# The opening, the window attention and the latent scores of an fp32 two-block kernel, rearranged together

## The chip, the cores and the metric

The kernel runs on one core of one Trainium2 chip. Its time is the device time of one execution in microseconds (us), the median of several runs. TensorE (PE) multiplies, VectorE (DVE) and ScalarE (ACT) do the elementwise work, GpSimd (POOL) some of it, and SyncE (SP) issues most of the transfers. PE's results lie in PSUM, in eight banks of 128 x 512 fp32 numbers.

## The reference

Two transformer blocks over 512 tokens of 1024 channels, all in fp32. The parts that the change touches:

```python
def rmsnorm(x, g):
    y = xf * lax.rsqrt(jnp.mean(xf * xf, axis=-1, keepdims=True) + NORM_EPS)
    return (y * g.astype(jnp.float32)).astype(x.dtype)
...
    h = jnp.concatenate([meta, x], axis=1)                   # 16 + 512 tokens
    h = h + 0.5 * swiglu(rmsnorm(h, ffn1_norm[i]), ffn1_w1[i], ffn1_w3[i], ffn1_w2[i])
    hn = rmsnorm(h, mix_norm[i])
    q, k, v, u, g_attn, g_ssm = jnp.split(hn @ w_in[i], SPLITS, axis=-1)
    attn = sliding_window_attention(q, k, v, attn_sinks[i])  # 16 heads of 64, window 128
...
def mla_mixer(...):                                          # 16 heads, queries in blocks of 128
    q_rope = apply_rope(q[..., MLA_NOPE:], cos[:, :, None], sin[:, :, None])
    k_rope = apply_rope(k_r, cos, sin)
...
        s = (jnp.einsum('bqhd,bkhd->bhqk', q_nope[:, q0:q1], k_nope[:, :q1])
             + jnp.einsum('bqhr,bkr->bhqk', q_rope[:, q0:q1], k_rope[:, :q1])).astype(jnp.float32) * scale
        s = jnp.where(mask[:, None], s, NEG_INF_2)
        pr = jax.nn.softmax(s, axis=-1).astype(v.dtype)
        outs.append(jnp.einsum('bhqk,bkhd->bqhd', pr, v[:, :q1]))
```

The rest (a state-space branch, gated FFNs with a convolution, a second, gated linear attention, layer norms and projections) is the same before and after.

## The kernel before

**Products.** The channels lie on the partitions, the tokens along them. A product of two fp32 matrices is made of three matmuls of fp32r operands, high by high, low by high and high by low part (`mm3`, L566 to L568). The weights of one output chunk of 128 columns, 8 input chunks deep, are a unit (128 x 1024); a raw tile (128 x 8 x 256) holds two. 24 matmuls (8 input chunks of three) make one 512-token output chunk in one bank, and 48 make the 528-token chunks of the first FFN, in two halves of 264. SP brings each raw tile into one of three raw buffers (`loads`, L501), ACT writes its high part `uh` (`feed_hi` or `ahead_hi`, L539), DVE the low part `ul` (`feed_lo` or `ahead_lo`, L554), and PE waits for both. "Ahead" means that a unit is prepared before the one in turn.

**Order.** Each engine has its own function for each stage (`..._pe`, `..._act`, `..._dve`, `..._sp`), and these write the engine's instructions in the order in which they run. Banks are taken in rotation by `Banks.take`; a taker waits until the last holder of the bank was read. `bk.limit(n, i)` makes the rotation run over n banks, from bank i on.

**Opening** (`setup_pe`, `setup_act`, `setup_dve`, `setup_sp`). The norm's gain rows of several layers come by nine transfers on ACT's queue into tile 0 of `vrows`, and PE turns all 112 at once into columns (`columns_pe`, L888). SP brings the input `xin` in eight pieces, four token blocks by two halves of the columns, with a semaphore for each block, then the first weights. PE turns the meta tokens (L902) and the eight input chunks (L908), DVE copies each to `H` (L933), ACT writes the gained high part `XH` (L813) and squares it (L772), DVE the low part `XL` (L820). After the fourth chunk ACT and DVE split the first two units (L539, L554). Only after all the transposes does PE begin the first unit, then the sums of squares (L751); ACT takes the root (L759), DVE the inverse (L766), and the first results are scaled out of the banks (L836).

**Window attention** (`window_pe`, `window_act`, `window_dve`). Sixteen attention steps (four groups of four heads, four query blocks n) run in a loop over i = 0 to 19: scores of i (`scores_pe`, L1756), softmax of i-1 (L1769, L1773 on DVE, L1786 on ACT), normalising of i-2 (L1803), turning of i-3 (`turn_pe`, L1821; copies L1837 on ACT and L1839 on DVE), values of i-4 (`values_pe`, L1850, and L1866 on DVE). Beside them the units for the queries of groups 1 to 3 and for their gates (`q`, `ga`), at the twelve steps of `WITH_UNIT`, and one unit `gs` at i = 17: each whole unit stands ahead of the turning and the scores of its step, and its result is scaled by L836. The banks 0 to 3 rotate, 4 to 7 hold the four heads' scores.

**Latent attention** (`latent_pe` and its fellows). Two heads are a pair p. Queries and keys of a pair come from three products (`queries_pe`: `qn`, `qr`, `kn`), ACT copies QN and KN out of the banks (L2282, L2286), DVE turns the rotary part (`rope_dve`: four copies of 32 partitions each, L2174, and three multiplications and additions, L2176 to L2180). The scores of a head (`latent_scores_pe`) are two fp32 matmuls for each query block n, of N = 128(n+1) keys: QN by KN (L2319) and the rotary rows of that head, QR by KR (L2320). Softmax is L2335 and L2338 on DVE, L2345 on ACT; turning is L2367, the values are L2395, and their output goes out by ACT (L2405) and DVE (L2409). The loop runs over i = 0 to 17, one head a step and a new pair at each even step.

## Time and profile before

| | us |
|---|---|
| median of three runs (2744.53 to 2750.54) | 2745.61 |
| the profiled execution | 2743.8 |
| its span, first to last instruction | 2742.0 |
| PE busy in it | 2676.6 |
| VectorE busy | 1674.5 |
| ScalarE busy | 1015.2 |
| GpSimd busy | 348.2 |

Times below are microseconds from the start of that span. The stages on its axis: the opening up to 44.2, the first FFN, the projections and the state-space branch up to 565.4, the window attention from 565.4 to 734.2, the rest of the first block and its FFN up to 1289.9 with the latent attention's first products at its end, the latent attention's loop from 1289.9 to 1578.8, and the rest up to 2742.0. A line "L566" is line 566 of the kernel. PEclk is the TensorE clock that was granted, as a share of full speed (1.00 is 2.4 GHz, 0.5 is 1.2 GHz). What stands in brackets behind an instruction is the idle time of its engine ahead of it and what ended that. The mark PEld is the weight load of a matmul, which runs beside the matmul ahead.

### The profile page before, as it was taken

The numbers are of one execution on the slowest core, as the hardware profiler recorded it, in microseconds if no ns is written. First come the engines' busy times: TensorE is split into PE (matmuls) and PEld (weight loads), VectorE is DVE, ScalarE is ACT, GpSimd is POOL, SyncE is SP. The second block draws the span as 40 slices with busy tenths as digits, with TensorE's granted clock in tenths as the row PEclk, the third lists the DMA queues.
The fourth block names the chain that finished last, engine by engine and source line by source line (L and its number), as shares of the span: only waits on it lengthen the run. The fifth ranks groups of instructions, "written<-read, shape, count | busy, mean of one in ns | idle before, by whom it ended". The sixth has DMA issues, their size and how long they took to land.

```text
span 2742.0 us, 35232 instructions
## 1 busy us (share of the span) xinstructions
PE 2676.6 (98%) x14595; PEld 2244.8 (82%) x14595; DVE 1674.5 (61%) x2553; ACT 1015.2 (37%) x1625; POOL 348.2 (13%) x361
## 2 busy tenths in 40 slices
PE   6999999988899999999999999999999999999999
PEld 6999999866687888887667688888887878888887
DVE  6754755668556544546664667737764467764765
ACT  3321333134334222333442435424454244542435
POOL 1133423020001000011000040000221014000031
PEclk9999999999899999999999999999999999999999
DMA  5243344421132233322111132332322212232231
GB/s 144 77 123 108 104 137 126 167 74 33 33 108 96 92 100 108 89 77 66 43 65 47 58 100 78 90 103 77 114 95 85 85 46 70 85 108 92 90 103 62
DMA packets 292727, 244.02 MB, mean 89 GB/s; under 512 B 19837, under 2 KB 285575, under 8 KB 292567
## 3 DMA queue, kind: packets, MB, share of 16 engines
q1 hardware_dynamic: 282503, 226.40, 26.1%
q0 software_dynamic: 5616, 13.22, 1.6%
q8 instruction: 115, 1.88, 0.3%
q10 hardware_dynamic: 4448, 2.16, 0.3%
q14 instruction: 45, 0.37, 0.0%
HBM read 230.70 MB, written 13.14 MB: 89 GB/s over the span
## 4 chain that ended last, share of the span: by engine, by line
PE 87%; DVE 8%; ACT 2%; issue 1%; DMA 1%; POOL 1%; ACTq 0%; SPq 0%; POOLq 0%; DVEq 0%
PE ps L566 26%; PE ps L567 25%; PE ps L568 25%; PE ps L2320 2%; PE ps L2319 2%; DVE ul L554 2%; PE ps L751 1%; PE ps L2395 1%; DVE rbuf L766 1%; PE ps L2367 1%; ACT S L1786 1%; ACT uh L539 1%; PE ps L3116 1%; PE ps L3092 1%; DVE tmp L2174 1%
## 5 line engine op out<-in xcount | busy, mean ns | idle before, releaser
L554 DVE TENSOR_TENSOR ul<-raw,uh 128x1024 fp32r<-128x1024 f32 (+3 forms) x416 | 526.5, 1289 | 340.5 <-ACT uh L539 340.1
L566 PE MATMUL ps<-OH,uh 128*128 128x512 f32 (+1 forms) x1736 | 646.6, 372 | 3.6 <-DVE ul L554 2.4
L568 PE MATMUL ps<-OH,ul 128*128 128x512 f32 (+1 forms) x1736 | 638.7, 368 | 0.0
L567 PE MATMUL ps<-OL,uh 128*128 128x512 f32 (+1 forms) x1736 | 638.5, 368 | 0.0
L539 ACT CAST uh<-raw 128x1024 fp32r<-128x1024 f32 (+3 forms) x416 | 411.9, 1025 | 158.3 <-PE ps L568 128.6
L566 PEld LDWEIGHTS ps<-OH,uh 128*128 128x128 f32 x1736 | 327.3, 189 | 66.6 <-issue 7.3
L567 PEld LDWEIGHTS ps<-OL,uh 128*128 128x128 f32 x1736 | 327.4, 189 | 55.2 <-issue 2.4
L568 PEld LDWEIGHTS ps<-OH,ul 128*128 128x128 f32 x1736 | 327.3, 189 | 54.6
L566 PE MATMUL ps<-XH,uh 128*128 128x264 f32 (+1 forms) x992 | 314.1, 317 | 13.4 <-DVE ul L554 8.1
L567 PE MATMUL ps<-HL,uh 128*128 128x512 f32 (+2 forms) x946 | 320.3, 339 | 0.0
L566 PE MATMUL ps<-HH,uh 128*128 128x512 f32 (+2 forms) x946 | 320.1, 338 | 0.0
L568 PE MATMUL ps<-HH,ul 128*128 128x512 f32 (+2 forms) x946 | 318.9, 337 | 0.0
L567 PE MATMUL ps<-XL,uh 128*128 128x264 f32 (+1 forms) x992 | 309.5, 312 | 0.0
L568 PE MATMUL ps<-XH,ul 128*128 128x264 f32 (+1 forms) x992 | 308.6, 311 | 0.0
L566 PEld LDWEIGHTS ps<-XH,uh 128*128 128x128 f32 x992 | 191.5, 193 | 31.1 <-DVE ul L554 8.8
L568 PEld LDWEIGHTS ps<-XH,ul 128*128 128x128 f32 x992 | 191.7, 193 | 9.1
L567 PEld LDWEIGHTS ps<-XL,uh 128*128 128x128 f32 x992 | 191.5, 193 | 8.5
L566 PEld LDWEIGHTS ps<-HH,uh 128*128 128x128 f32 x946 | 177.8, 188 | 22.8 <-issue 0.9
L567 PEld LDWEIGHTS ps<-HL,uh 128*128 128x128 f32 x946 | 177.7, 188 | 20.8 <-issue 0.5
L568 PEld LDWEIGHTS ps<-HH,ul 128*128 128x128 f32 x946 | 177.9, 188 | 19.7
L782 POOL TENSOR_TENSOR acc<-acc,tmp 128x512 f32<-128x512 f32 (+2 forms) x56 | 70.3, 1255 | 697.6 <-ACT tmp L772 693.1
L2552 POOL TENSOR_TENSOR acc<-H 128x512 f32<-128x512 f32 x4 | 8.6, 2149 | 974.3 <-DVE H L2791 623.2
(434 smaller groups left out, 3710.8 us busy)
## 6 DMA issues: line engine op xcount, KB each, us to landing
raw<-in_ffn_w SPq DMA_DIRECT2D x40, 1024.0 KB, 5.0
raw<-in_ffn_w_up SPq DMA_DIRECT2D x40, 1024.0 KB, 5.0
raw<-in_ffn_w SPq DMA_DIRECT2D x32, 704.0 KB, 4.3
raw<-in_ffn_w_down SPq DMA_DIRECT2D x32, 704.0 KB, 4.3
raw<-in_w_in SPq DMA_DIRECT2D x16, 1024.0 KB, 5.4
raw<-in_gla_w_in SPq DMA_DIRECT2D x12, 1024.0 KB, 5.0
raw<-in_mla_w_o SPq DMA_DIRECT2D x8, 1024.0 KB, 4.8
raw<-in_ple_w_gate SPq DMA_DIRECT2D x8, 1024.0 KB, 4.9
```

The costliest lines, as they stand in the source:

```text
L539: e.copy(h, src).then_inc(*s_whi.up((u, j)))
L554: e.tensor_tensor(l, src, h.bitcast(F32), SUB).then_inc(*s_wlo.up(("unit", u)))
L566: e.matmul(o, wh, xh, start=first, stop=False)
L567: e.matmul(o, wh, xl, start=False, stop=False)
L568: return e.matmul(o, wl, xh, start=False, stop=last)
L751: i = e.matmul(psum[:, b, 0:n], ones[:, :], tile[:, t0:t0 + n], start=j == 0, stop=j == len(parts) - 1)
L766: e.reciprocal(r[:, t0:t0 + n], r[:, t0:t0 + n]).then_inc(*s_dv.up((tag, "r", hf)))
L782: e.tensor_tensor(a, a, tmps[k - 1][:, t0:t0 + n], ADD).then_inc(*s_pool.up(*((tag, "acc", k, hf) for hf in hfs)))
L1786: e.activation(S_[:, r, 0:ntot], S_[:, r, 0:ntot], ACT.Exp, bias=z[:, 1, r:r + 1], accum_out=z[:, 3, r:r + 1]).then_inc(*s_fn.up())
L2174: e.tensor_copy(s[32 * k:32 * k + 32, :], P(key, 512, slice(32 * (k ^ 1), 32 * (k ^ 1) + 32))).then_inc(*s_dv.up())
L2319: e.matmul(psum[:, b, 0:N], QN[:, hh, 128 * n:128 * n + 128], KN[:, hh, 0:N], start=True, stop=False)
L2320: e.matmul(psum[:, b, 0:N], QR[p0:p0 + 64, 128 * n:128 * n + 128], KR[p0:p0 + 64, 0:N], start=False, stop=True).then_inc(*s_mm.up(("ms", h ...
```

## The change

**1, the opening.** The first norm's gain gets an 8-row tile of its own (`g1row`, turned to `g1`), whose transfer is the first on ACT's queue; the other rows of tile 0 are turned later, in `norm()`, with tiles 1 to 3. The input has one semaphore for each half of its columns in place of one for each token block. SP brings the first half, the meta tokens, the first weight, the second half and the second weight. ACT runs one small activation ahead of its work. PE turns chunks 0 and 1, the meta tokens, chunks 2 and 3, and then takes the first unit input chunk by input chunk, with the turning of chunks 4 to 7 between. The splitting of the first unit is one unit long, the second unit is split after the last chunk. After the sums of squares the banks start again at 0 of 8.

**2, the window attention.** The units are no longer whole: `along_pe` runs them in pieces of input chunks, `CHUNKS[i]` of them at step i, those that go on with a begun unit ahead of the turning, those that begin one behind the scores (`lin_piece`). They have bank 3 alone, and 0 to 2 rotate for the rest. `gs` is the last of them. DVE adds up the values (i-4) ahead of normalising (i-2), and splits the next unit ahead of the copy from the turning or behind it (`soon`).

**3, the latent scores.** Each pair of fp32 matmuls becomes five of fp32r: three for the plain part (high and low of QN and KN) and two for the rotary part, QA by the high and the low part of KR, where QA holds the high part of the head's rotary query in one half of its partitions and the low part in the other. N is at least 256. ACT writes the high parts (QNH, KNH, QA) and takes over the four copies of the rotary part (`rope_act`); DVE subtracts for the low parts (QNL, KNL, QA's other half). KR is split once.

The diff, cut to its core:

```diff
+def lin_piece(e, name, X, t0, n, key, bank, k0, k1):
+    xh, xl, tag = X
+    if k0 == 0:
+        piece_of[key] = next_unit(e, name)
+        bk.take(e, key, bank)
+    u = piece_of[key]
+    hi, lo, _ = halves_of(u)
+    for k in range(k0, k1):
+        s_lo.wait_ge(e, (tag, k))
+        i = mm3(e, psum[:, bk.of[key], 0:n], hi[:, k, :], lo[:, k, :], xh[:, k, t0:t0 + n],
+                xl[:, k, t0:t0 + n], k == 0, k == 7)
+    if k1 == 8:
+        i.then_inc(*s_mm.up(key, ("unit", u)))
+piece_of = {}
...
         cs = slice(512 * half, 512 * half + 512)
         for i in range(4):
...
+            loads(e, 1)
     loads(e, 2)
...
+def turn_input_pe(e, c):
+    b = bk.take(e, ("xt", c))
+    d_x[c // 4].wait_ge(e, "x")
+    for i in range(4):
+        t = e.transpose(psum[:, b, i * 128:(i + 1) * 128], xin[:, i, c * 128:(c + 1) * 128], ident[:, :])
+    t.then_inc(*s_mm.up(("xt", c)))
...
 def setup_pe(e):
     s_cst.wait_ge(e, "ident")
-    columns_pe(e, 0)
+    b = bk.take(e, "g1")
+    d_g1.wait_ge(e, "row")
+    e.transpose(psum[:, b, 0:8], g1row[:, :], ident[0:8, 0:8]).then_inc(*s_mm.up("g1"))
+    for c in range(2):
+        turn_input_pe(e, c)
     b = bk.take(e, "xm")
...
-    for c in range(8):
-        b = bk.take(e, ("xt", c))
-        for i in range(4):
-            d_x[i].wait_ge(e, c // 4)
-            t = e.transpose(psum[:, b, i * 128:(i + 1) * 128], xin[:, i, c * 128:(c + 1) * 128], ident[:, :])
-        t.then_inc(*s_mm.up(("xt", c)))
+    for c in range(2, 4):
+        turn_input_pe(e, c)
+    u = next_unit(e, "f1")
+    keys = [("F1", "a", 0, hf) for hf in range(2)]
+    for key in keys:
+        bk.take(e, key)
+    hi, lo, _ = halves_of(u)
+    for k in range(8):
+        if k < 4:
+            turn_input_pe(e, 4 + k)
+        s_lo.wait_ge(e, ("ffn1", k))
+        for (t0, n), key in zip(H1, keys):
+            i = mm3(e, psum[:, bk.of[key], 0:n], hi[:, k, :], lo[:, k, :], XH[:, k, t0:t0 + n],
+                    XL[:, k, t0:t0 + n], k == 0, k == 7)
+            if k == 7:
+                i.then_inc(*s_mm.up(key, *([("unit", u)] if key == keys[1] else [])))
...
 def setup_act(e):
+    e.dma_start(g1row[:, :], r8(A["ffn1_norm"][0])).then_inc(*d_g1.up("row"))
...
-    s_dv.wait_ge(e, ("col", 0))
+    s_cst.wait_ge(e, "ones")
+    e.activation(misc[:, 3:4], one, ACT.Identity, scale=one).then_inc(*s_fn.up())
+    s_dv.wait_ge(e, "g1")
...
+    ahead_hi(e, 1)
...
-    s_dv.wait_ge(e, ("col", 0))
...
+        if c == 4:
+            feed_lo(e, "f1", 0)
...
-        if c == 5:
-            feed_lo(e, "f1")
...
+    ahead_lo(e, 1)
...
-        for tile in range(1, 4):
+        bk.limit(8, 0)
+        for tile in range(4):
             columns_pe(e, tile)
...
+ALONG = [("q" if n < 2 else "ga", 2 * g + n % 2) for g in range(1, 4) for n in range(4)] + [("gs", 0)]
+CHUNKS = (8, 8, 8, 7, 7, 7, 6, 6, 6, 6, 6, 6, 5, 5, 5, 3, 2, 2, 1, 0)
+def pieces_of(i, rest):
+    a = sum(CHUNKS[:i])
+    b = a + CHUNKS[i]
+    x = [(u, max(a - 8 * u, 0), min(b - 8 * u, 8)) for u in range(len(ALONG)) if a < 8 * u + 8 and b > 8 * u]
+    return [p for p in x if (p[1] > 0) == rest]
+def begun(i):
+    return [ALONG[u] for u, _, _ in pieces_of(i, False)]
+def ended(i):
+    x = (pieces_of(i - 1, False) if i else []) + pieces_of(i, True)
+    return [ALONG[u] for u, _, k1 in x if k1 == 8]
+def soon(i):
+    return sum(k1 - k0 for _, k0, k1 in pieces_of(i, True)) < 3
+def along_pe(e, i, rest):
+    for u, k0, k1 in pieces_of(i, rest):
+        name, c = ALONG[u]
+        lin_piece(e, name, MIX, 16, 512, (name, c, 0), 3, k0, k1)
...
-    bk.limit(4)
+    bk.limit(3)
...
-        if q_ga(i):
-            name, c = q_ga(i)
-            lin(e, name, MIX, HR, (name, c))
...
+        along_pe(e, i, True)
         if 3 <= i <= 18:
             turn_pe(e, i - 3)
         if i < 16:
             scores_pe(e, i)
+        along_pe(e, i, False)
...
+        if 3 <= i <= 18 and soon(i):
+            turn_copy(e, i - 3, True)
...
+        for name, c in ended(i - 1) if i else ():
+            ga_act(e, name, c)
+        for name, c in begun(i):
+            feed_hi(e, name)
+        if 3 <= i <= 18 and not soon(i):
             turn_copy(e, i - 3, True)
...
+        if i >= 4:
+            values_dve(e, i - 4)
...
-        if i >= 4:
-            values_dve(e, i - 4)
-        if q_ga(i):
-            feed_lo(e, q_ga(i)[0])
-        if i == 17:
-            feed_lo(e, "gs")
+        if not soon(i):
+            for name, c in begun(i):
+                feed_lo(e, name)
+        for name, c in ended(i):
+            if name == "gs":
+                scale_dve(e, ("gs", 0, 0), tmps[0][:, 0:512], rmix, ("gs in", 0))
+            else:
+                q_ga_dve(e, name, c)
         if 3 <= i <= 18:
             turn_copy(e, i - 3, False)
-        if i == 17:
-            scale_dve(e, ("gs", 0, 0), tmps[0][:, 0:512], rmix, ("gs in", 0))
-        if q_ga(i):
-            q_ga_dve(e, *q_ga(i))
+        if soon(i):
+            for name, c in begun(i):
+                feed_lo(e, name)
...
+def rope_act(e, key):
     s_mm.wait_ge(e, key)
+    if key[0] == "qr" and key[1] > 2:
+        s_dv.wait_ge(e, ("rope", "qr", key[1] - 3, 0))
+    for k in range(4):
+        e.copy(rope_tile(key)[32 * k:32 * k + 32, :], P(key, 512, slice(32 * (k ^ 1), 32 * (k ^ 1) + 32))).then_inc(
+            *s_cp.up(("rope",) + key))
...
-        e.copy(QN[:, hh, :], P(("qn", p, hh, 0))).then_inc(*bk.free(s_cp, ("qn", p, hh, 0), ("qn", p, hh)))
-    feed_hi(e, "uk", 1 if p == 1 else 2)
+        e.copy(QNH[:, hh, :], P(("qn", p, hh, 0))).then_inc(*s_hi.up(("qn", p, hh)))
+    rope_act(e, ("qr", p, 0))
...
+        e.copy(KNH[:, hh, :], P(("kn", p, hh, 0))).then_inc(*s_hi.up(("kn", p, hh)))
...
+def queries_turned_act(e, p):
+    s_dv.wait_ge(e, ("rope", "qr", p, 0))
+    for hh in range(2):
+        rows = slice(64 * hh, 64 * hh + 64)
+        e.copy(QA[rows, hh, :], QR[rows, :]).then_inc(*s_hi.up(("qr", p, hh)))
+    feed_hi(e, "uk", 1 if p == 1 else 2)
...
-            s_dv.wait_ge(e, ("rope", "qr", p - 3, 0))
...
+        s_lo.wait_ge(e, "KR")
+    for hh in range(2):
+        s_hi.wait_ge(e, ("qn", p, hh))
+        e.tensor_tensor(QNL[hh][:, :], P(("qn", p, hh, 0)), QNH[:, hh, :].bitcast(F32), SUB).then_inc(
+            *bk.free(s_lo, ("qn", p, hh, 0), ("qn", p, hh)))
...
+        s_hi.wait_ge(e, ("kn", p, hh))
+        e.tensor_tensor(KNL[:, hh, :], P(("kn", p, hh, 0)), KNH[:, hh, :].bitcast(F32), SUB).then_inc(
...
+def queries_turned_dve(e, p):
+    for hh in range(2):
+        rows, other = slice(64 * hh, 64 * hh + 64), slice(64 - 64 * hh, 128 - 64 * hh)
+        s_hi.wait_ge(e, ("qr", p, hh))
+        e.tensor_tensor(QA[other, hh, :], QR[rows, :], QA[rows, hh, :].bitcast(F32), SUB).then_inc(
+            *s_lo.up(("qr", p)))
...
-    p, hh, p0 = h // 2, h % 2, 64 * (h % 2)
-    s_cp.wait_ge(e, ("kn", p, 1))
-    s_dv.wait_ge(e, ("rope", "qr", p, 0))
-    s_dv.wait_ge(e, "KR")
+    p, hh = h // 2, h % 2
...
+    s_lo.wait_ge(e, "KR")
+    s_lo.wait_ge(e, ("qr", p))
     for n in range(4):
-        N = 128 * (n + 1)
+        N = max(128 * (n + 1), 256)
         b = bk.take(e, ("ms", h, n), 4 + n)
-        e.matmul(psum[:, b, 0:N], QN[:, hh, 128 * n:128 * n + 128], KN[:, hh, 0:N], start=True, stop=False)
-        e.matmul(psum[:, b, 0:N], QR[p0:p0 + 64, 128 * n:128 * n + 128], KR[p0:p0 + 64, 0:N], start=False,
-                 stop=True).then_inc(*s_mm.up(("ms", h, n), ("ms", h)))
+        o, q = psum[:, b, 0:N], slice(128 * n, 128 * n + 128)
+        mm3(e, o, QNH[:, hh, q], QNL[hh][:, q], KNH[:, hh, 0:N], KNL[:, hh, 0:N], True, False)
+        e.matmul(o, QA[:, hh, q], KRH[:, 0:N], start=False, stop=False)
+        e.matmul(o, QA[:, hh, q], KRL[:, 0:N], start=False, stop=True).then_inc(
+            *s_mm.up(("ms", h, n), ("ms", h)))
```

How the change stands in the engines' order. A row is a line of the kernel, the operation, result<-operands and the result's shape, with the count where rows repeat.

**The first places on PE.** Before, from its first instruction (`vrows` are the gain rows, `xme` the meta tokens, `xin` the input, `uh` and `ul` the parts of the first weight):

```order
L888 MATMUL ps<-ident,vrows 128x112
L902 MATMUL ps<-ident,xme 128x16 x8
L908 MATMUL ps<-ident,xin 128x128 x32
L566 MATMUL ps<-XH,uh 128x264
L567 MATMUL ps<-XL,uh 128x264
L568 MATMUL ps<-XH,ul 128x264
L566 MATMUL ps<-XH,uh 128x264
```

After (`g1row` is the first norm's own row tile):

```order
L933 MATMUL ps<-ident,g1row 128x8
L924 MATMUL ps<-ident,xin 128x128 x8
L939 MATMUL ps<-ident,xme 128x16 x8
L924 MATMUL ps<-ident,xin 128x128 x12
L572 MATMUL ps<-XH,uh 128x264
L573 MATMUL ps<-XL,uh 128x264
L574 MATMUL ps<-XH,ul 128x264
L572 MATMUL ps<-XH,uh 128x264
L573 MATMUL ps<-XL,uh 128x264
L574 MATMUL ps<-XH,ul 128x264
L924 MATMUL ps<-ident,xin 128x128 x4
L572 MATMUL ps<-XH,uh 128x264
```

Four of the input chunks went from ahead of the first product to between its steps of six matmuls; the meta tokens stand behind two chunks.

**SP's queue at the start**, before and after:

```order
L846 DMA xin<-in_x 128x512 x4
L848 DMA xme<-in_meta_tokens 16x1024
L846 DMA xin<-in_x 128x512 x4
L501 DMA raw_49<-in_ffn_w 128x8x256
L501 DMA raw_50<-in_ffn_w 128x8x256
```

```order
L869 DMA xin<-in_x 128x512 x4
L871 DMA xme<-in_meta_tokens 16x1024
L507 DMA raw_49<-in_ffn_w 128x8x256
L869 DMA xin<-in_x 128x512 x4
L507 DMA raw_50<-in_ffn_w 128x8x256
```

One weight tile went ahead of the second half of the input.

**DVE at step 4 of the window attention**, from the scores of step 3's softmax (`S`) to the state-space side work (`U`); `Mg` is the attention's output, `PT` the turned weights, `Q` the scaled query. Before:

```order
L1769 SCALAR_TENSOR_TENSOR S_121<-ps,mk_123 128x1088
L1773 TENSOR_REDUCE sst<-S_121 128x4
...
L1803 TENSOR_TENSOR S_128<-S_120,sst 128x4x16
L1803 TENSOR_TENSOR S_120<-S_120,sst 128x4x128
L1866 SCALAR_TENSOR_TENSOR Mg<-Mg,ps 128x128 x2
L554 TENSOR_TENSOR ul<-raw_50,uh 128x1024
L1839 COPY PT<-ps 128x512
L836 TENSOR_TENSOR Q<-ps,mbuf 128x512
L1702 SCALAR_TENSOR_TENSOR U<-U,cv,tmp_62 128x8x66
```

After:

```order
L1842 SCALAR_TENSOR_TENSOR S_123<-ps,mk_125 128x1088
L1846 TENSOR_REDUCE sst<-S_123 128x4
...
L1939 SCALAR_TENSOR_TENSOR Mg<-Mg,ps 128x128 x2
...
L1876 TENSOR_TENSOR S_130<-S_122,sst 128x4x16
L1876 TENSOR_TENSOR S_122<-S_122,sst 128x4x128
L560 TENSOR_TENSOR ul<-raw_50,uh 128x1024
L859 TENSOR_TENSOR Q<-ps,mbuf 128x512
L1912 COPY PT<-ps 128x512
L1756 SCALAR_TENSOR_TENSOR U<-U,cv,tmp_62 128x8x66
```

The adding of the values went ahead of the normalising, and the result of the unit ahead of the copy from the turning.

**DVE at a new pair of heads in the latent attention** (`ps` is a bank, `tmp` the rotary part's tile). Before:

```order
L554 TENSOR_TENSOR ul<-raw_50,uh 128x512
L554 TENSOR_TENSOR ul<-raw_51,uh 128x512
L2174 COPY tmp_62<-ps 32x512 x4
L2176 TENSOR_TENSOR QR<-ps,COS 128x512
L2178 TENSOR_TENSOR tmp_62<-tmp_62,SIN 128x512
L2180 TENSOR_TENSOR QR<-QR,tmp_62 128x512
L554 TENSOR_TENSOR ul<-raw_49,uh 128x4x256
L554 TENSOR_TENSOR ul<-raw_49,uh 128x4x128
L2409 TENSOR_TENSOR OL<-ps,OH 128x512
L2387 COPY PTm<-ps 128x512
```

After:

```order
L560 TENSOR_TENSOR ul<-raw_50,uh 128x512
L560 TENSOR_TENSOR ul<-raw_51,uh 128x512
L2394 TENSOR_TENSOR QNL_158<-ps,QNH 128x512
L2394 TENSOR_TENSOR QNL_159<-ps,QNH 128x512
L2258 TENSOR_TENSOR tmp_58<-ps,COS 128x512
L2260 TENSOR_TENSOR tmp_62<-tmp_62,SIN 128x512
L2262 TENSOR_TENSOR tmp_58<-tmp_58,tmp_62 128x512
L2399 TENSOR_TENSOR KNL<-ps,KNH 128x512 x2
L2521 TENSOR_TENSOR OL<-ps,OH 128x512
L2406 TENSOR_TENSOR QA<-tmp_58,QA 64x512 x2
L560 TENSOR_TENSOR ul<-raw_49,uh 128x4x256
```

The four copies left DVE; six subtractions came, four of them of 128 x 512 and two of 64 x 512, and the output's subtraction (`OL`) stands between them.

**PE at a head's scores.** Before, six of eight:

```order
L2319 MATMUL ps<-KN,QN 128x128
L2320 MATMUL ps<-KR,QR 128x128
L2319 MATMUL ps<-KN,QN 128x256
L2320 MATMUL ps<-KR,QR 128x256
L2319 MATMUL ps<-KN,QN 128x384
L2320 MATMUL ps<-KR,QR 128x384
```

After, the first seven of twenty:

```order
L572 MATMUL ps<-KNH,QNH 128x256
L573 MATMUL ps<-KNL,QNH 128x256
L574 MATMUL ps<-KNH,QNL_158 128x256
L2431 MATMUL ps<-KRH,QA 128x256
L2432 MATMUL ps<-KRL,QA 128x256
L572 MATMUL ps<-KNH,QNH 128x256
L573 MATMUL ps<-KNL,QNH 128x256
```

Five matmuls stand where two stood, and the narrowest has 256 columns.

## Rows read from the trace of the kernel before

**Rows 1.** The page: busy time of each engine.

```profile
PE 2676.6 (98%) x14595; PEld 2244.8 (82%) x14595; DVE 1674.5 (61%) x2553; ACT 1015.2 (37%) x1625; POOL 348.2 (13%) x361
```

**Rows 2.** By stage: length, busy of PE, PEld, DVE, ACT, POOL, PEclk, DMA.

```profile
0.00:44.20 44.20, 23.46 (x124) 21.49 (x124) 23.61 (x30) 17.13 (x24) 11.54 (x19) 0.85 0.64 175
...
565.40:734.20 168.80, 146.05 (x795) 105.88 (x793) 120.43 (x245) 67.92 (x203) 8.33 (x16) 0.92 0.12 35
...
1289.90:1578.80 288.90, 285.78 (x1235) 195.27 (x1233) 178.20 (x345) 112.91 (x266) 0.00 (x0) 1.00 0.15 51
```

**Rows 3.** Chain of waits at the opening: start, duration, what.

```profile
4.16 5.95 DMA vrows<-in_ple_b_gate
...
21.65 3.89 DVE ul L554 x2
...
29.96 1.62 DVE XL L820
...
40.40 3.46 DVE rbuf L766 x2
```

**Rows 4.** PE's timeline at the opening: start, duration, what, [idle <-releaser].

```profile
11.56 6.17 PE L908 MATMUL ps<-ident,xin 128*128 128x128 f32 x32
23.35 0.59 PE L566 MATMUL ps<-XH,uh 128*128 128x264 f32 x1 [5.62 <-DVE ul L554]
...
37.46 0.61 PE L751 MATMUL ps<-acc,ones 128*128 128x264 f32 x2
...
44.20 0.39 PE L566 MATMUL ps<-XH,uh 128*128 128x264 f32 x1 [1.58 <-DVE tmp L836]
```

**Rows 5.** Transfers of the input issued from 2.0 to 2.5 us.

```profile
DMA to landing us min/median/max: 4.3/4.5/4.8
```

**Rows 6.** PE's waits, 571 to 742 us: us in all, times, longest.

```profile
PE ps L1850 <- ACT PT L1837: 7.9, 3, 4.0
```

**Rows 7.** PE's timeline at a turning, a step's scores and values.

```profile
706.53 0.38 PE L1816 MATMUL ps<-ident,S 128*64 128x128 f32 x2
...
707.28 0.28 PE L1756 MATMUL ps<-KS,Q 64*128 64x16 f32 x1
...
708.69 0.59 PE L1850 MATMUL ps<-PT,VB 64*128 64x256 f32 x2
...
709.80 0.41 PE L1816 MATMUL ps<-ident,S 128*64 128x128 f32 x2
```

**Rows 8.** PE's timeline behind the window attention.

```profile
734.72 0.63 PE L567 MATMUL ps<-YL,uh 128*128 128x512 f32 x1
735.15 0.63 PE L568 MATMUL ps<-YH,ul 128*128 128x512 f32 x1
```

**Rows 9.** DVE's groups in the window attention: busy, mean ns | idle before.

```profile
L554 DVE TENSOR_TENSOR ul<-raw,uh 128x1024 fp32r<-128x1024 f32 x12 | 14.7, 1225 | 17.6 <-ACT uh L539 17.6
```

**Rows 10.** PE's timeline of one head's scores, and the next pair's first.

```profile
1348.04 0.39 PE L2319 MATMUL ps<-KN,QN 128*128 128x128 f32 x2
...
1353.81 0.70 PE L2395 MATMUL ps<-PTm,VT 128*128 128x512 f32 x1
...
1380.75 0.39 PE L2319 MATMUL ps<-KN,QN 128*128 128x128 f32 x2
```

**Rows 11.** PE's timeline of fp32r matmuls, 256 and 512 columns.

```profile
1343.75 0.28 PE L566 MATMUL ps<-uh,CKH 128*128 128x256 f32 x1
1343.87 0.28 PE L567 MATMUL ps<-ul,CKH 128*128 128x256 f32 x1
...
1336.03 0.39 PE L567 MATMUL ps<-CQL,uh 128*128 128x512 f32 x1
1336.25 0.39 PE L568 MATMUL ps<-CQH,ul 128*128 128x512 f32 x1
```

**Rows 12.** DVE's and ACT's groups in the latent attention.

```profile
L2174 DVE COPY tmp<-ps 32x512 f32<-32x512 f32 x28 | 19.2, 687 | 28.4 <-PE ps L568 27.7
...
L2282 ACT COPY QN<-ps 128x512 f32<-128x512 f32 x14 | 8.1, 582 | 11.5 <-PE ps L568 11.5
```

88 lines of the change are left out of this document (45 added, 43 removed).

## The prediction, made before the changed kernel ran

> **What bounds the kernel now.** I read the busy table first: PE is at work 2676.6 us of a span of 2742.0, so 65.4 us are idle, and whatever else a change does, it must either fill that idle time or take work from PE [rows 1]. The table by stage says where both are to be had: the opening has 20.7 us without PE work in 44.2, the window attention 22.75 in 168.8 at a granted clock of 0.92, and the latent loop only 3.1 in 288.9 at a clock of 1.00 [rows 2]. Those three are the three stages that the change touches. Then I read the chain of waits and PE's timeline for the opening, PE's waits for the window, and the steps between starts of matmuls for the latent scores, since matmuls overlap in the records and only the distance of their starts is a price.
>
> **1, the opening.** Before, nothing on PE starts until the last of nine row transfers is down, 4.16 + 5.95 = 10.1 us [rows 3]; the first input chunk is turned from 11.56 on [rows 4]. The first half of the input is there long before: its last piece is issued shortly after 2.0 us and lands 4.8 later, at 6.9 [rows 5]. After, only the norm's own rows, first on ACT's queue, stand ahead, so turning starts at about 7.0, 4.5 us earlier. I then walk along DVE, which makes the chain. Before, it ends with XL at 29.96 + 1.62 = 31.6 [rows 3]. Take away the 4.5, and half of the 3.89 us in which DVE split two weights in the middle (now one there, the other behind) [rows 3]: 25.2. But chunks 4 to 7 are now turned behind the wait for the split weight and at PE's pace. With PE at its lower clock, where 512 columns take 0.43 [rows 8], 264 take 0.22, and a chunk's six matmuls 1.3, with 0.8 for its turning (32 small matmuls took 6.17, four take 0.77) [rows 4]. That puts about 3.4 back: XL is done at 28.6. What is gained behind that is larger: before, most of the first product (31.6 to 37.46) ran after the chain [rows 3, 4], after, only the last chunk's six matmuls are left, and the sums of squares begin at 29.4 in place of 37.46, 8.1 earlier. The wait of 1.58 at 44.20 for a bank [rows 4] stands behind two halves of a product in place of one; the inverse of 3.46 [rows 3] still has to pass, now with one more weight split on DVE ahead of it. I count 0.9 for it. **Opening: 9.0 less.** If PE never leaves the lower clock there, 48 matmuls of 0.22 and four turnings take 13.8 us from the end of the first split on (21.65 + 3.89 before [rows 3], 4.5 and 1.9 less now: 19.1), to 33 and not 29.4, and 5 are left; if the 3.4 does not arise, 12. The weight now ahead of the input's second half delays that half, but chunk 4 is not wanted before 19.
>
> **2, the window attention.** The floor is what PE has to do at full clock. 13 units of 24 matmuls of 0.23 [rows 11] are 73; a turning takes 0.75 with one band block and 1.2, as an estimate by its twelve small matmuls in place of six or so, with two; scores 1.41; values 1.11 to 1.6 [rows 7]; over 16 steps some 60. That gives 133.6, beside 146.05 busy [rows 2]: the 12.4 between is work done at the lower clock, as in the products right behind the stage, which step by 0.43 where 0.23 is full speed [rows 8, 11]. With the 22.75 of idle the stage is 35.2 above its floor. The longest waits are those of the values for the turned weights, 7.9 us in three [rows 6]: in the steps without a unit there is nothing to put between. I split the 35.2 by place: about 10 in the tail behind the last scores (708.7 to 734.2, 25.5 us for 15.4 of work [rows 7]), 25 before it. After, every step up to 18 has some chunks between, 5 to 8 of them in the first fifteen, and each full step takes PE about 9.2. DVE's share of a step is 120.43 / 16 = 7.5 [rows 2], and it is under 9.2, but it waits 17.6 us for ACT's high parts ahead of its own [rows 9]; 7.5 and 1.1 make 8.6, still under. So the loop should run near PE's pace, with short waits where a begun unit stands behind scores and its split comes last, and where a third bank of the turning must be freed by the copy (three banks rotate and not four). By a walk of the first fifteen steps those leave 12 of the 25. The tail keeps its chain of softmax, normalising, turning and values with only 5 chunks to put between; I give it 20 and not 25.5, as the first of its waits is gone. 133.6 + 12 + 4.6 = 150.2 beside 168.8: **window 18.5 less.** Bounds: 28, where only half of the tail's 10 stay and the clock does not fall before it; 8, where the waits move and do not shrink and the clock still falls in them.
>
> **3, the latent scores.** A head's scores take 1353.81 - 1348.04 = 5.77 us, a pair of heads 1380.75 - 1348.04 = 32.7 [rows 10]. An fp32r matmul of 256 columns steps by 0.12, of 512 by 0.22 to 0.23 [rows 11], and 384, which I put between, by 0.17. Five for each block of queries, at 256, 256, 384 and 512 columns: 5 x (0.12 + 0.12 + 0.17 + 0.23) = 3.2. So PE saves 2.58 a head, 41.3 over 16 heads, and a pair falls from 32.3 (32.7 less a wait of 0.4 that each pair has) to 27.1 of PE work. The cost is on the others. DVE loses four copies of 0.687 a pair [rows 12] and gets six subtractions of about the same length (a subtraction of the same free size as the copy; of 64 partitions as long as of 128), 1.4 more: of some 22 a pair (178.2 over the stage [rows 2]) 23. ACT gets the four rotary copies and two for QA at 0.58 [rows 12], 3.5 more on 14. Both stay under 27, but the order has a new zigzag, ACT's copies, DVE's three rotary steps, ACT's QA, DVE's QA, ahead of the scores of the new pair, with the output's low part in the same queue: 2.3 + 2.1 + 1.2 + 1.4 = 7 us. PE's products and turning stand beside it, and by the walk a pair keeps about 1.0 of waits: 28.1, 4.6 less. Six periods of it are 27.6, the first and the last pair give 3.9 and 5.2, and behind the last scores, with no queries of a next pair to run, 3.5 come back as waits: **latent 33 less.** Bounds 22 and 39 (the 41.3 less a tail of 2). Splitting KR once is one operation of 0.6 on each engine, beside PE's products: nothing, or 1 if the first scores wait for it.
>
> **Sum.** The profiled execution took 2743.8 (its span and 1.8 around it), the median is 1.8 higher, inside the runs' spread of 6. 2743.8 - 9.0 - 18.5 - 33 = 2683.3, rounded to 2684.
>
> **The rivals.**
> Both loops reach PE's floor: window 28 and latent 39 to 41 less, with 9 for the opening, 2666. For it speaks that DVE is busy 7.5 of 9.2 and 23 of 27.1, against it that both loops have zigzags between two engines. 0.12.
> The window's gain is lost: the chain through softmax on DVE, exponentials on ACT and back decides each step, and pieces only move the waits. Then at most 8 there: 2694. For it, the 17.6 us for which DVE waited on ACT [rows 9]; against it, in the steps that had a unit PE hardly waited. 0.13.
> The latent loop becomes bound by DVE and the zigzag: a pair takes 31 and not 28, gain 16 to 18: 2701. 0.10.
> The opening's order does not do what it says (a transfer of the row tile or of the half as late as before): that costs up to 9 and stays in the range, 2693. 0.02.
> Slower: PE's clock. The waits get shorter and more frequent, with one or more in each step of both loops, and should the chip answer these with its lower clock, the loops' 134 and 217 us of PE work run partly at half speed. Forecast gains of 60 and 5 more are used up when 0.19 of that work is so, a granted clock of 0.9 and less over both loops; fully low pairs cost 27 us each, and three of eight do it: over 2750. Against it: the clock was 1.00 through the latent loop, whose pairs each had a short wait, and low in the window only where waits were 2 to 5 us long [rows 2, 6]. 0.03.
> The Trainium skill, "TensorE: Matmul & The Clock Gate", section "A second HAM failure mode: psum-queue depth-cycling", tells of a kernel whose short idle times between groups of matmuls, as its banks cycled, let the clock swing between its two levels. By that rule this last rival would be the result; the trace of before, with 1.00 in the loop that has such waits, does not agree so far.
>
> **How the numbers follow.** The forecast, 2684, has 0.60. Its own bounds are 2666 to 2703 if all three parts went the same way, which they need not. The range of 2664 to 2704 takes in the floor, the lost window and most of the bound latent loop; some 0.15 to 0.2 is left out. A measurement of this kernel can tell about 0.2% (5.5 us). No case but the last ends above 2740: faster 0.97, same 0.01, slower 0.02.
>
> **What would show it.** Right: PE's first turning at about 7, the sums of squares near 29 to 30; the window stage at 150 with a clock nearer to 1 and no wait of the values over 2 us before the tail; pairs of 28 us with 1 us of waits, a head's scores 3.2 us long, the QA subtraction or OL as releaser. Wrong: a PE clock under 0.95 in the latent loop, DVE idle for ACT by more than 3 us a pair, a step of the window longer than 10 us, or matmuls of 128 x 256 that step by more than 0.12 when five different weights follow one another.

## The result: 2686.62 us, and the profile after

The changed kernel takes 2686.62 us, the median of four runs (2684.73 to 2688.15), beside 2745.07 for the kernel before. The ratio is 0.9782, with a 95% interval of 0.9765 to 0.9799: 58.5 us less between the medians. 2684 had been forecast. The profiled execution took 2688.15, its span is 2686.3. In a later batch one of nine executions of the kernel before took 4974.91 us, and it is left out of the ratios.

The page of the changed kernel, its busy times, to be read against [rows 1]:

```profile
PE 2628.2 (98%) x14660; PEld 2247.4 (84%) x14660; DVE 1677.2 (62%) x2567; ACT 1040.7 (39%) x1679; POOL 346.4 (13%) x361
```

PE has 48 us less work and 7 us less idle time. DVE, which lost the rotary part's copies and won the low parts' subtractions, is where it was, and ACT has 26 us more. The same stages as in [rows 2], cut at the same events (columns: length, busy of PE, PEld, DVE, ACT, POOL, PEclk, DMA share, GB/s):

```profile
0.00:35.40 35.40, 20.16 (x125) 18.39 (x126) 20.72 (x27) 17.64 (x25) 10.60 (x19) 1.00 0.77 216
35.40:557.30 521.90, 517.27 (x4110) 502.42 (x4108) 322.16 (x576) 144.83 (x195) 146.00 (x166) 0.98 0.38 118
557.30:711.60 154.30, 140.89 (x793) 99.99 (x793) 120.77 (x245) 67.63 (x203) 8.33 (x16) 0.99 0.13 38
711.60:1268.00 556.40, 554.84 (x2421) 454.32 (x2422) 286.85 (x351) 184.69 (x247) 28.03 (x20) 0.99 0.30 94
1268.00:1523.10 255.10, 245.10 (x1299) 206.20 (x1297) 183.42 (x359) 132.33 (x308) 0.00 (x0) 0.99 0.18 58
```

The opening's end is the start of the second half of the second product; the window attention begins with the last scaling on DVE ahead of the loop and ends with the first product of the state-space output; the loop goes from the first latent scores to the first product of its output projection. Cut there, every kernel gives a column of this table, which I made from the timelines, with the cuts rounded to 0.1 us (by this cut the window stage of the kernel before is 168.5 and not the 168.8 of [rows 2]). "After again" is the changed kernel in a second profile, "the last version" the one at the end of the experiments:

| stage, us | before | after | after again | opening alone | window alone | scores alone | the last version |
|---|---|---|---|---|---|---|---|
| opening | 44.2 | 35.4 | 35.5 | 35.3 | 44.1 | 43.9 | 34.5 |
| first FFN, projections | 521.5 | 521.9 | 522.8 | 517.0 | 520.6 | 520.4 | 520.7 |
| window attention | 168.5 | 154.3 | 154.2 | 168.6 | 154.4 | 168.4 | 151.1 |
| to the first latent scores | 555.7 | 556.4 | 556.2 | 555.9 | 555.8 | 555.8 | 555.9 |
| latent loop | 288.9 | 255.1 | 255.2 | 288.9 | 289.0 | 255.1 | 252.4 |
| the rest | 1163.2 | 1163.2 | 1163.2 | 1163.2 | 1163.2 | 1163.3 | 1162.7 |

So 8.8 us came from the opening, 14.2 from the window, 33.8 from the latent loop, and 1.1 went back in the two stretches between: 55.7, the difference of the two spans.

**The opening** in the changed kernel, PE's timeline (start, duration, what, [idle <- releaser]), against [rows 4]:

```profile
7.76 1.97 PE L924 MATMUL ps<-ident,xin 128*128 128x128 f32 x8 [4.58 <-DMA xin<-in_x]
...
18.70 1.11 PE L924 MATMUL ps<-ident,xin 128*128 128x128 f32 x4 [6.12 <-DVE ul L560]
...
22.17 0.28 PE L574 MATMUL ps<-XH,ul 128*128 128x264 f32 x1
22.29 0.29 PE L572 MATMUL ps<-XH,uh 128*128 128x264 f32 x1
...
29.36 0.60 PE L774 MATMUL ps<-acc,ones 128*128 128x264 f32 x2
```

Turning starts at 7.76, not at 11.56, and now waits for the input. From 22.17 on the matmuls step by 0.12, PE's full speed; ahead of it they step by 0.22, at the lower clock. (The clock's record begins at 22.07 in this trace, so the PEclk of 1.00 in the opening's row says nothing of the time before.) In the kernel before the record begins at 16.64, and of the 20.5 us from there to 37.12 PE had the lower clock for 13.7. The sums of squares start at 29.36, not at 37.46.

**The window's waits** in the changed kernel (engine and line, whom they waited for: us in all, times, longest), against [rows 6]:

```profile
PE ps L572 <- DVE Q L859: 4.7, 2, 2.4
PE ps L1923 <- ACT PT L1910: 2.3, 3, 0.8
PE ps L1923 <- DVE PT L1912: 1.7, 1, 1.7
```

The values' waits for the turned weights (L1923) are small now. New is the first row: a unit that begins waits for bank 3, which the scaling of the finished unit must free.

**The latent loop**: PE's timeline of one pair's start, against [rows 10]; a head's scores run from 1345.74 to 1349.03, 3.29 us. The last row is the next pair's turning, 27.72 later:

```profile
1344.67 1.31 PE L2479 MATMUL ps<-ident,SS 128*128 128x128 f32 x10 [0.82 <-ACT VT L2418]
1345.74 0.36 PE L572 MATMUL ps<-KNH,QNH 128*128 128x256 f32 x1
...
1349.03 1.34 PE L2507 MATMUL ps<-PTm,VT 128*128 128x512 f32 x3
...
1372.39 0.87 PE L2479 MATMUL ps<-ident,SS 128*128 128x128 f32 x6 [0.82 <-ACT VT L2418]
```

Such a pair has one wait, 0.8 us for VT, the copies of the values' product, on ACT. Four of the pairs are so; the others wait at other places: 1.4 for KNL and 1.6 for QA in the first pair, 1.4 for a low part in the stretch with the first half of the output projection, and 2.3 for OL at the end.

### The profile page after: what moved, and what is told of

It is laid out like the page before. It is cut to its first block, busy times and chain, and to the rows that moved or that the text cites. A ratio compares the mean times of both kernels' runs of the same rounds, so it can differ in the third digit from the quotient of the medians.

```text
span 2686.3 us, 35439 instructions
## 1 busy us (share of the span) xinstructions
PE 2628.2 (98%) x14660; PEld 2247.4 (84%) x14660; DVE 1677.2 (62%) x2567; ACT 1040.7 (39%) x1679; POOL 346.4 (13%) x361
## 4 chain that ended last, share of the span: by engine, by line
PE 87%; DVE 7%; ACT 3%; issue 1%; DMA 1%; POOL 1%; SPq 0%; ACTq 0%; POOLq 0%; DVEq 0%
PE ps L572 27%; PE ps L573 26%; PE ps L574 26%; PE ps L774 1%; DVE ul L560 1%; PE ps L2507 1%; ACT uh L545 1%; PE ps L2479 1%; PE ps L3232 1%; PE ps L3208 1%; DVE rbuf L789 0%; PE ps L1589 0%; ACT S L1859 0%; PE ps L1927 0%; PE ps L1829 0%
## 5 line engine op out<-in xcount | busy, mean ns | idle before, releaser
L573 PEld LDWEIGHTS ps<-OL,uh 128*128 128x128 f32 x1736 | 327.4, 189 | 55.7 <-issue 2.4
```

Of the source, the lines that this page charges most:

```text
L573: e.matmul(o, wh, xl, start=False, stop=False)
```

## The experiments

### The three parts alone

Each is the kernel before with the hunks of one part. (Where an experiment further down has no median, it ran once, and it is read by the lengths of its stages.)

> The kernel before with the change's opening alone. Theory (the three parts are independent, each gains what its stage shows in the trace of the changed kernel): the stage up to the second half of the first norm's second product, 44.2 us before, takes 35.3, and what follows is the kernel before's, so about 8.9 less, 0.3%; the 0.9 us that the stretch behind it was longer in the changed kernel comes with it, so 8 to 9 less in the total. Rival (a stage's gain is partly handed on to the next wait): under 6 less. Second point: PE's turning starts at 7.8 and the sums of squares at 29.4, as in the changed kernel.

Measured: 2732.52 us (2727.33 to 2733.77) beside 2743.03 on that chip, ratio 0.9964 (0.9949 to 0.9978). The opening is 35.3, the sums of squares start at 29.25.

> The kernel before with the change's window attention alone. Theory: its stage falls from 168.8 to 154.2 us, 14.6 less in the total, with the waits for Q and Mg of 2.4, 2.3, 0.9, 0.8 and 0.6 us at begun units, as in the changed kernel. Rival (the clock of the stage depends on what ran before it): the granted clock of the stage is not 0.99 but nearer to the 0.92 of before, and 8 us or less are gained.

Measured: 2730.20 (2723.95 to 2733.70), ratio 0.9954 (0.9938 to 0.9970). The window stage is 154.4, with the same waits as in the changed kernel, 4.7 us of them for Q.

> The kernel before with the split scores alone. Theory: from the first scores to the first product behind the loop 288.8 us become 254.7, 34 less, and the stretch ahead of the loop 1 longer, so 33 less in the total, a pair of heads 27.7. Rival (the parts help each other): 25 less or fewer, or over 40.

Measured: 2710.42 (2707.11 to 2713.14), ratio 0.9884 (0.9866 to 0.9901). The loop is 255.1 and the stretch ahead of it 0.1 longer, so the 0.7 that the changed kernel has there is not this part's.

The parts are independent: by the ratios they give 9.9, 12.6 and 31.8 us, together 54, each give or take some 4, and by the stages each has to within 0.3 us what it has in the whole. The rivals, that a stage hands its gain on or that the parts help each other, are out, and so is a window stage with a clock near the 0.92 of before: it was 0.98.

### Which rows the opening waited for

> The changed kernel with the transfer of the norm's own rows issued last of the nine on ACT's queue and not first. Theory (PE's first turning needs these rows only by the order of its queue; now it starts at 7.8 us with the input): it starts at 10 to 10.5, and the sums of squares move from 29.4 to about 32, 2.5 later. Rival (the chain behind is bound by the weight's split or the second half of the input and absorbs the start): they stay within 0.5 us of 29.4.

```diff
-e.dma_start(g1row[:, :], r8(A["ffn1_norm"][0])).then_inc(*d_g1.up("row"))
 for r, n, ap in vparts[0]:
     e.dma_start(vrows[r:r + n, 0, :], ap).then_inc(*d_vr[0].up("rows"))
+e.dma_start(g1row[:, :], r8(A["ffn1_norm"][0])).then_inc(*d_g1.up("row"))
```

Its timeline of PE at the start and at the sums of squares:

```profile
10.46 0.24 PE L933 MATMUL ps<-ident,g1row 8*128 8x8 f32 x1 [10.46 <-DMA g1row<-in_ffn_norm]
10.63 1.97 PE L924 MATMUL ps<-ident,xin 128*128 128x128 f32 x8
...
32.26 0.61 PE L774 MATMUL ps<-acc,ones 128*128 128x264 f32 x2
```

2.9 us later in turning, 2.9 later at the sums: the start of the turning is handed on in full, and the order of the rows is worth a third of the opening's 8.8. The other 5.9 I put down to the first product, which now runs beside the chain; no run takes that apart. (The total is 2688.13, that of the first profile: the opening is 2.9 longer, the window stage 4.0 longer and the stretch between them 6.6 shorter, in code that this edit does not touch; that is the next point.)

### The scaling ahead of the split

> The changed kernel with one swap on DVE in the window attention: the finished unit's scaling (Q, Mg) ahead of the split of the unit that begins. Theory: PE's waits for Q (2.4 and 2.3 us at 613.9 and 650.2) and for Mg (0.8, 0.6) at the start of a unit come from the scaling standing behind a split that itself waits for ACT's cast; with the swap those four waits go, as bank 3 is free earlier, and the lower clock that follows the second of them (9 matmuls in 3.9 us and not 2.0) goes too: 5 to 8 less than the changed kernel. Rival (the weight's split is what PE really needs at that place): the same waits appear on the split part, and the time stays within 2 us.

```diff
-if not soon(i):
-    for name, c in begun(i):
-        feed_lo(e, name)
 for name, c in ended(i):
     ...
+if not soon(i):
+    for name, c in begun(i):
+        feed_lo(e, name)
```

Measured: 2681.52 (2680.53 to 2682.70), ratio 0.9779 (0.9763 to 0.9796). The window stage is 151.1. The first of PE's waits in it, and those for Mg at the start of a unit:

```profile
PE ps L1923 <- DVE PT L1912: 2.8, 3, 1.7
PE ps L1923 <- ACT PT L1910: 2.5, 4, 0.8
...
PE ps L572 <- DVE Mg L859: 1.3, 2, 0.7
```

Both waits for Q are gone; those for Mg, which I had put to the same cause, stayed, and PT's grew by 1.3. Of 5 to 8 us expected 3.2 came beside the first profile of the changed kernel, whose window stage is of the short kind, and 7.2 beside those in which it takes 158.3 (below); the medians are 5.1 apart, and 7.4 from the changed kernel's later one. The theory is right for Q and wrong for Mg.

How much it is worth depends on the clock. After both waits for Q the changed kernel does this (first profile):

```profile
613.88 0.47 PE L572 MATMUL ps<-XH,uh 128*128 128x512 f32 x1 [2.41 <-DVE Q L859]
614.19 0.40 PE L573 MATMUL ps<-XL,uh 128*128 128x512 f32 x1
...
650.18 0.76 PE L572 MATMUL ps<-XH,uh 128*128 128x512 f32 x1 [2.25 <-DVE Q L859]
650.74 0.63 PE L573 MATMUL ps<-XL,uh 128*128 128x512 f32 x1
651.17 0.63 PE L574 MATMUL ps<-XH,ul 128*128 128x512 f32 x1
```

The first is followed by steps of 0.23, full clock, the second by steps of 0.43, the lower one. In the run with the rows last, whose window code is the same, the first is followed by steps of 0.43 too:

```profile
610.24 0.77 PE L572 MATMUL ps<-XH,uh 128*128 128x512 f32 x1 [2.42 <-DVE Q L859]
610.80 0.63 PE L573 MATMUL ps<-XL,uh 128*128 128x512 f32 x1
```

and the ten microseconds around it have a granted clock of 0.56, those of the changed kernel 1.00 (columns as in the table by stage; first the changed kernel, then the other):

```profile
612.00:622.00 10.00, 8.12 (x40) 5.82 (x40) 8.74 (x16) 4.59 (x14) 4.16 (x8) 1.00 0.49 134
```

```profile
608.00:618.00 10.00, 7.76 (x21) 4.58 (x22) 6.88 (x12) 4.79 (x14) 4.17 (x8) 0.56 0.48 134
```

Added up over the window stage, the time at the lower clock is 28.0 us in each of the three profiles with the old window code, 3.4 to 3.6 in three of the new code (stage 154.3), 7.1 in the window-alone run (154.4, where one wait of 0.9 at the stage's start is missing), and 13.9 in the other five (158.3 to 158.4), with the same waits in all. By the two waits for Q: behind the second, of 2.2 to 2.3 us, the clock fell for 3.4 us in all nine profiles. Behind the first, of 2.4, it stayed in three, fell for 3.4 in one and for 10.2 in five, and this makes the 4.1 us between 154.3 and 158.4. With Q's waits gone the lower clock takes 3.7 and 3.9 us, in the tail, and the stage 151.1.

The same goes on ahead of the window, in code that no experiment there touched, where the stretch is 515.3 to 522.8 us long. Its length goes with the time at the lower clock in it, over all fourteen profiles (of both kernels and the twelve runs of this part) by some 0.4 us for each microsecond: 3.4 us at the lower clock with the rows last (515.3 long), 6.8 with the opening alone (517.0), 10.2 with the scaling first (518.5), and 17.1 and 20.5 in the two profiles of the changed kernel (521.9 and 522.8). The two stretches are tied in some way: the three profiles whose clock stayed behind the first wait for Q are those with 521.2 to 522.8 here, the one with a short fall has 520.6, and the five with the long fall have 515.3 to 519.5. Forty microseconds of it, the changed kernel first, then the rows last:

```profile
510.00:550.00 40.00, 37.08 (x206) 31.69 (x206) 19.64 (x43) 9.31 (x15) 11.38 (x25) 0.83 0.48 145
```

```profile
508.00:548.00 40.00, 37.40 (x256) 32.69 (x255) 20.44 (x44) 10.55 (x18) 11.51 (x25) 1.00 0.48 146
```

Nor does a fall need a wait. Ahead of the latent loop, 3.5 to 7 us before its first scores, the clock falls for 3.4 or 6.8 us in each of the fourteen profiles, and in the 7 us before that fall PE was never idle for longer than 0.15. What sets a fall and its length I did not find, nor did I try anything in this stretch.

### Narrower scores

> The changed kernel with the scores of the first query block at N = 128 keys and not 256. Theory (an fp32r matmul's time goes by its columns, 0.12 us for 256 and 0.23 for 512 in the trace): a step of 0.06, so 0.3 less a head and 4.8 less over 16. Rival (a narrow fp32r matmul runs at the fp32 pair's rate, 0.2 to 0.3 us for 128 columns): 0.6 to 0.9 more a head, 10 to 14 more.

```diff
-N = max(128 * (n + 1), 256)
+N = 128 * (n + 1)
```

The loop is 255.2, not changed. PE's timeline of the first blocks of a head:

```profile
1503.27 0.27 PE L574 MATMUL ps<-KNH,QNL 128*128 128x128 f32 x1
1503.38 0.28 PE L2431 MATMUL ps<-KRH,QA 128*128 128x128 f32 x1
...
1503.89 0.28 PE L574 MATMUL ps<-KNH,QNL 128*128 128x256 f32 x1
1504.01 0.28 PE L2431 MATMUL ps<-KRH,QA 128*128 128x256 f32 x1
```

128 columns step by 0.11, 256 by 0.12. Neither theory holds: a matmul with a weight of its own hardly gets shorter below 256 columns here, nor longer. The wide first block costs next to nothing: a pair is 27.67 with the narrow one and 27.71 to 27.74 without. (The clock fell in other places in this run, 1.5 us more in the first pair behind waits of 1.4 and 1.6, 1.1 less in the last, so the equal lengths of the loops are in part chance, and the pairs are the better measure.)

### Who holds the latent pair

> The changed kernel with the rotary part's four copies back on DVE, as in the kernel before. Theory (the pair is bound by PE, and DVE waits 2.1 us for these copies anyway): DVE's chain ends 0.7 us later in a pair, and the loop of 255.1 us gets 0 to 6 longer. Rival (DVE is the bound of the new loop): 2.75 us more in each of eight pairs, 22 longer. Other rival (the change's own choice is wrong, ACT's share causes the VT wait): shorter by 3 or more.

```diff
 def rope_dve(e, key, dst):
     s = rope_tile(key)
-    s_cp.wait_ge(e, ("rope",) + key)
+    s_mm.wait_ge(e, key)
...
+    for k in range(4):
+        e.tensor_copy(s[32 * k:32 * k + 32, :], P(key, 512, slice(32 * (k ^ 1), 32 * (k ^ 1) + 32))).then_inc(
+            *s_dv.up())
```

The loop is 264.6, 9.5 longer, between the first theory's 0 to 6 and the rival's 22; a pair is 28.55 us (1347.06 to 1375.61) with a wait of 1.0 for DVE's KNL:

```profile
1347.06 0.39 PE L572 MATMUL ps<-uh,CKH 128*128 128x256 f32 x1 [0.97 <-DVE KNL L2398]
...
1375.61 0.39 PE L572 MATMUL ps<-uh,CKH 128*128 128x256 f32 x1 [1.01 <-DVE KNL L2398]
```

But 4.9 of the 9.5 stand in the first pair (33.6 and not 28.7), and the clock has most of them: from a wait of 2.1 on it fell for 10.2 us, and one head's scores took 6.0 us, from the first of these lines to the second, where 3.3 is full speed:

```profile
1291.86 0.58 PE L572 MATMUL ps<-KNH,QNH 128*128 128x256 f32 x1 [1.34 <-DVE QA L2405]
...
1297.90 2.41 PE L2506 MATMUL ps<-PTm,VT 128*128 128x512 f32 x8
```

PE worked 7.9 us at the lower clock there; at half of that, 4.0, the copies themselves are worth 5.5, by this estimate, which is within the first theory. The stretches behind the first pair are 0 to 1.6 longer. So moving the four copies to ACT carries 5.5 to 9.5 of the loop's 33.8, as the clock falls or not. DVE is near its limit without being busy all the time: the order in which it stands between PE and ACT is.

> The changed kernel with one move on ACT in the latent loop: for pairs 2 to 7 the four copies of the values' product (VT) stand ahead of the casts of the next two weights, and not behind them. Theory: the wait of 0.8 us that PE now has once in four of the pairs (turning, for VT) comes from the two casts, 1.56 us, ahead of the copies, because ACT got six more instructions a pair; it goes, and the loop from the first scores on, 255.1 us, is 3 to 4 shorter. Rival (the copies from the turning, PTm, behind DVE's later split, take its place): the wait appears at the values or the turning under another name and the loop stays within 1 us.

```diff
 def queries_turned_act(e, p):
     ...
+    if p >= 2:
+        values_copied(e, p - 1)       # the four copies of VT
     feed_hi(e, "uk", 1 if p == 1 else 2)
```

The theory fell. The wait for VT went, but the loop is 261.8, 6.7 longer (some 1.7 of it, by estimate, is a fall of the clock for 3.4 us behind the wait of 2.8 for a low part, which the changed kernel does not have there); PE's waits in it:

```profile
PE ps L572 <- DVE OL L2531: 7.1, 5, 3.0
PE ps L572 <- DVE ul L560: 2.8, 1, 2.8
```

and DVE's timeline in a pair shows why: it stands 1.36 us for the cast that ACT now makes behind VT, and everything behind it comes that much later, OL last:

```profile
1344.43 1.83 DVE L560 TENSOR_TENSOR ul<-raw,uh 128x1024 fp32r<-128x1024 f32 x2 [1.36 <-ACT uh L545]
```

The next two runs try the two ways out of this.

> The changed kernel with two edits in different stages. Opening: the first weight's transfer stands behind the second half of the input again. Theory (the weight is wanted by ACT at 16.5 us, the second half at 18.7, and both are down before that in either order): the sums of squares stay where they are, 28.6 to 29.7; rival (the first half of the input lands earlier or later by what follows it in the queue): 0.5 or more. Latent loop: ACT's copies of VT ahead of the casts (as in the run that made the loop 261.8) and DVE's split of those weights behind its copies from the turning. Theory (that run lost because the later cast held DVE's whole chain 1.4 us back, up to OL, not because of VT): the loop is back to 255 or shorter, 251 at best. Rival (the loss came from ACT's other work standing later): 259 or more.

```diff
 (DVE, latent loop)
-    feed_lo(e, "uk", 2)
-    feed_lo(e, "uv")
     latent_turn_copy(e, i - 2, False)
+    feed_lo(e, "uk", 2)
+    feed_lo(e, "uv")
```

The loop is 257.4: 4.4 of the 6.7 came back, so the late cast was most of the cause. The 2.3 that stay are in one place: the stretch with the first half of the output projection is 3.8 longer than the changed kernel's, with a wait of 2.8 for a low part where that has 1.4, and steps of 0.43 for some 3 us behind it; the other pairs together are 1.5 shorter. Opening: the sums of squares at 29.07, after turning from 7.51 on; the same 21.6 between as in the changed kernel. The place of the weight's transfer makes no difference.

> The changed kernel with two edits in different stages. Opening: input chunk 4 is turned ahead of the wait for the first weight's low part, not behind it. Theory (behind the split the chain waits 1.1 us for PE's turning, 18.70 to 19.82, before DVE can copy chunk 4): the sums of squares begin about 1 us earlier than the 28.6 to 29.7 of the runs so far; rival (DVE's chain of copies and XL is the bound, PE is not): under 0.4. Latent loop: for pairs 2 to 7 ACT's casts of the next two weights stand ahead of the output's cast, where ACT waits 1.0 to 1.4 us for PE, so that nothing stands between QA and VT. Theory (0.8 of wait in four or five pairs is ACT's order alone, and DVE's chain, which gave 7 us more when VT was put ahead of the casts, is not delayed by this): the loop falls from 255.1 to 251.5 to 252.5. Rival (DVE is the bound of a pair in either order): 254.5 or more.

```diff
 def queries_act(e, p):
     ...
+    if p >= 2:
+        feed_hi(e, "uk", 2)
 def queries_turned_act(e, p):
     ...
-    feed_hi(e, "uk", 1 if p == 1 else 2)
+    if p < 2:
+        feed_hi(e, "uk", 1 if p == 1 else 2)
```

The loop is 252.5, as expected. The first rows of the view of its PE waits, from 6 us ahead of the loop to 15 us behind it (the second wait for OL, 0.7, lies behind the loop):

```profile
PE ps L572 <- DVE OL L2525: 3.2, 2, 2.5
PE ps L572 <- DVE QA L2410: 1.6, 1, 1.6
PE ps L572 <- DVE ul L560: 1.5, 1, 1.5
PE ps L2483 <- DVE KNL L2403: 1.4, 1, 1.4
```

None of these recurs in each pair; a pair is 26.7 to 27.1 us and PE waits for no more than 0.4 us at a time in it. ACT had two casts to do and 1.4 us of idle time in front of the output's cast; they stand there now. The opening's edit was not tried by this run: the wait for the first weight stands in `next_unit`, ahead of the turning that I had moved, and PE's order was the same as in the changed kernel.

### A version with all of it, and the changed kernel again

> The changed kernel with three orders altered: the window's scaling ahead of the next unit's split on DVE (window stage 151.1 where it was alone), ACT's casts of the next weights ahead of the output's cast in the latent loop (252.5 where it was alone), and the fifth input chunk turned ahead of everything that waits for the first weight; in the earlier run that wait stood ahead of the turning all the same, so the opening's edit was not tried there. Theory: the stages add up, window 151, loop 252.5, sums of squares at 28.0 to 28.6 (1.1 less after the same start), and the time is 6 to 9 less than the changed kernel's beside it, with less spread, since the two waits of 2.3 us are gone after which the clock fell in some runs and not in others. Rival: a stage's gain is given back in another stage, under 3 in all.

The three edits together, and chunk 4 turned ahead of `next_unit`:

```diff
-    u = next_unit(e, "f1")
     keys = [("F1", "a", 0, hf) for hf in range(2)]
     for key in keys:
         bk.take(e, key)
+    turn_input_pe(e, 4)
+    u = next_unit(e, "f1")
     hi, lo, _ = halves_of(u)
     for k in range(8):
-        if k < 4:
+        if 0 < k < 4:
             turn_input_pe(e, 4 + k)
```

> The changed kernel itself, beside the version above, on one chip with the kernel before. Theory: 0.978 of the kernel before, and in the profile the window stage is either 154.3 or 158.4 us long with the same waits, by whether the clock falls once or twice in it. Rival: the differences of the window stage between runs are those of the experiments' edits, and it is 154.3 here.

Measured: 2680.01 us (2678.93 to 2682.44), ratio 0.9774 (0.9754 to 0.9794), beside 2688.94 (2684.63 to 2690.46), ratio 0.9799 (0.9780 to 0.9818), for the changed kernel on the same chip: 8.9 us between the medians, and the slowest of the one below the fastest of the other. Window 151.1, loop 252.4, as alone. In the opening, turning from 7.14 and the sums at 28.43 are 21.3 apart and not 21.6: 0.3, where I expected 1.1. (The same opening code gave 21.55 to 21.64 in six other profiles and 22.0 in two.) PE turned chunk 4 at 13.64 while it waited, but then ran the product at the lower clock up to past 21.5, and where DVE had waited 1.2 for chunk 4 and 0.8 for chunk 5, it now waited 0.9 for chunk 5 and 0.8 for chunk 6:

```profile
13.64 1.09 PE L924 MATMUL ps<-ident,xin 128*128 128x128 f32 x4 [1.67 <-DMA xin<-in_x]
18.09 0.59 PE L572 MATMUL ps<-XH,uh 128*128 128x264 f32 x1 [3.37 <-DVE ul L560]
...
21.53 0.42 PE L574 MATMUL ps<-XH,ul 128*128 128x264 f32 x1
```

In the repeated run of the changed kernel the window stage is 154.2, with one fall of the clock in it, behind the second wait for Q. The range of five runs is 3.5 us for the version and 5.8 for the changed kernel.

## Why the prediction was right, and where its terms were off

The forecast was 2684, measured 2686.62; the sum of gains was 60.5, measured 55.7 in the spans. That the total is only 2.6 off where the gains are 4.8 off is luck: the forecast was counted down from one profiled execution and rounded up, and the changed kernel's median lies 1.5 below its own profiled one. By its steps:

- **The opening, 9.0 forecast, 8.8 measured.** The parts of the walk hold too: turning at 7.0 (7.76; the transfer took 5.6 and not 4.8), the end of the split at 19.1 (18.7), the sums at 29.4 (29.36). One assumption was wrong without harm: I kept PE at its lower clock through the chunks (and yet gave the last chunk's six matmuls 0.8 where that clock takes 1.3), and it rose at 22.2. The bound of 5 for a clock that never rises was not needed.
- **The window, 18.5 forecast, 14.2 measured.** The mechanism was right, and so was the floor for the kernel before. With each matmul priced by the mean step of its kind at full clock, the stage before has 134.5 us of PE work, 73.4 in the units and 61.1 in the small steps, where I had 133.6, 73 and some 60; the 11.2 up to its 145.7 busy is the lower clock's, where I had 12.4. The term that I put at nothing is what the cutting of the units costs PE: the same matmuls take 138.9 in the changed kernel, 4.4 more, 2.9 of them in the units. There are 27 stretches of unit matmuls and not 13, and each begins with a longer step and often ends with one:

```profile
604.17 0.39 PE L574 MATMUL ps<-XH,ul 128*128 128x512 f32 x1
604.49 0.70 PE L1923 MATMUL ps<-PT,VB 64*128 64x256 f32 x2
...
606.13 0.50 PE L572 MATMUL ps<-XH,uh 128*128 128x512 f32 x1
606.46 0.39 PE L573 MATMUL ps<-XL,uh 128*128 128x512 f32 x1
606.70 0.39 PE L574 MATMUL ps<-XH,ul 128*128 128x512 f32 x1
```

The step into the values is 0.32 and the first step of the piece 0.33, where one within a piece is 0.23. A second way of counting agrees: the busy time of the stage, less half of what PE did at the lower clock, is 134.3 in the three profiles with the old window code and 138.8 to 139.4 in the eleven with the new. No run tried fewer pieces, so the price is read from the traces and not taken away by an edit. The idle time fell from 22.7 to 13.4 and the lower clock's price from 11.2 to 2.0; above the floor of each I had 35.2 and 16.6, and it was 34.0 and 15.4. What stays behind is about what I forecast but elsewhere: the two waits for Q of 2.4 and 2.3 us, because DVE's scaling stands behind a split that itself waits for ACT's cast, were no more in the text than "short waits where a begun unit stands behind scores", and the lower clock follows one or both of them (without both the stage is 3.2 shorter than with a fall behind the second alone). The tail went from 25.5 to 21.7 (689.9 to 711.6), where I had 20.
- **The latent loop, 33 forecast, 33.8 measured.** A head's scores 3.2 (3.29), a pair 28.1 (27.7), PE's work 41.3 less (40.6 by its busy time), DVE's load 23 (22.4) and ACT's 17.5 (16.7). The wait that a pair keeps is 0.8 and not 1.0, and not at QA or OL, which I named, but at VT on ACT, behind two casts: the engine I held for the free one. The end gave back what I had put down, 2.3 of it at OL. The rival in which DVE bounds the loop is nearer than it looked from its busy share: with four copies more on DVE 9.5 us go, with one cast late 6.7, though some 4 and 1.7 of these are the clock's.
- **Between the stages**, where I had nothing, 0.4 and 0.7 went back. The first is within what that stretch varies by itself, and none of the parts alone shows the second.
- **The slower rival**, a clock that falls with many short waits, did not come: the clock of the loops is 0.99 in both. In the window every fall stands at a wait of 1.5 us or more, and in the latent loop at one of 1.6 or more; behind the pairs' waits of 0.8 none came in six profiles. The rule of the Trainium skill that I set beside it ("TensorE: Matmul & The Clock Gate", section "A second HAM failure mode: psum-queue depth-cycling") is not borne out by these loops.
- **The bounds** were added up wrongly: the smallest gains, 5, 8 and 22, are 35 together and make 2709, not 2703, and a latent gain of 16 to 18 makes 2698 to 2700, not 2701. The measured time is far from both.

## What to carry to other kernels

Cut every kernel at the same events and compare the lengths of the stages: here they repeat to 0.3 us where the clock does not fall, while totals scatter by 6, and edits in different stages can be read from one run; but compare the time at the lower clock of a stage first, for a fall of 10 us makes 4 us of length that are not the edit's. When work is moved off a crowded engine, look at what it lands ahead of: ACT was 52% busy in the latent loop and still held PE up in its pairs, since two casts that nobody wanted yet stood ahead of a copy that PE wanted; and the cure was not to put the wanted copy first but the casts into idle time, as the crowded engine hung on both. A wait of some 2 us on TensorE may be worth more than its length, as the clock may fall behind it. And work that is cut into pieces to fill waits is not free: here 14 more pieces go with 4.4 us more of the engine's time, against 18.6 won in idle time and clock.

## What the runs showed of the hardware

- After one and the same wait of 2.4 us the granted clock of PE stayed at full in three profiles, fell for 3.4 us in one and for 10.2 in five; this made 4.1 us of the window stage. After another of 2.2 to 2.3 us it fell for 3.4 in all nine. The length of the stretch ahead of the window, 515.3 to 522.8, goes with 3.4 to 20.5 us at the lower clock. In the latent loop's pairs, with waits of 0.8 us, the clock stayed at 1.00; ahead of that loop it fell in all fourteen profiles though PE had not been idle.
- Unit matmuls of 512 columns step by 0.23 us, and the first of a piece, behind values, by 0.33: the cut of 13 units into 27 pieces, with the other switches between kinds of matmul (74 and not 59), goes with 4.4 us more of PE work at full clock.
- An fp32r matmul with its own weight of 128 columns steps by 0.11 us at 128 moving columns, 0.12 at 256, 0.17 to 0.18 at 384 and 0.23 at 512.
